# Feed-forward blocks of a two-layer hybrid decoder step: order of the TensorE passes in each slice's first output, and place of the sums of squares

## The reference

```python
def rms_norm(x, g):
    xf = x.astype(jnp.float32)
    y = xf * lax.rsqrt(jnp.mean(xf * xf, axis=-1, keepdims=True) + EPS)
    return (y * g.astype(jnp.float32)).astype(x.dtype)

def sqrelu_mlp(h, w_up, w_down):
    return jnp.square(jax.nn.relu(h @ w_up)) @ w_down

xp = xp + op
xp = xp + sqrelu_mlp(rms_norm(xp, norm_mlp[i]), mlp_w_up[i], mlp_w_down[i])
```

## Time and profile before

| | before |
|---|---|
| median of 3 runs | 2505.18 us (2504.93 to 2505.47) |
| profiled execution, its own time | 2504.88 us |
| its span | 2502.7 us |
| PE busy | 2414.7 us, 96% |
| DVE busy | 1013.8 us, 41% |
| ACT busy | 574.8 us, 23% |
| POOL busy | 107.1 us, 4% |
| DMA, mean | 61 GB/s |
| mean granted clock of PE | 0.987 |

### The profile page before, as it was taken

The page is one execution under the profiler, slowest core; times in us unless marked ns, Lnnn a source line. Parts: engine busy times, 40 slices in busy tenths (PEclk is TensorE's granted clock), DMA queues, the critical chain, the costliest instruction groups (busy, mean ns, idle before and its releaser), DMA issues.

```text
span 2502.7 us, 35278 instructions
## 1 busy us (share of the span) xinstructions
PE 2414.7 (96%) x15189; PEld 2339.8 (93%) x15189; DVE 1013.8 (41%) x1391; ACT 574.8 (23%) x998; POOL 107.1 (4%) x121
## 2 busy tenths in 40 slices
PE   6997899999999999999999998999999999999998
PEld 6995689999999999999999998888999999999998
DVE  5346833533333334334622323644433333333333
ACT  5346832201101111102410014522110110110111
POOL 0003510000000000000000002200000000000000
PEclk9998999999999999999999999999999999999999
DMA  8522021111111111111221126432111111111111
GB/s 227 106 48 76 2 88 51 34 51 34 50 34 50 50 34 50 37 47 50 88 54 51 34 76 181 122 109 84 34 50 50 34 50 42 42 50 34 50 34 70
DMA packets 122486, 153.86 MB, mean 61 GB/s; under 512 B 24797, under 2 KB 97273, under 8 KB 122120
## 3 DMA queue, kind: packets, MB, share of 16 engines
q1 hardware_dynamic: 116732, 139.33, 18.4%
q0 software_dynamic: 2832, 13.08, 1.8%
q10 hardware_dynamic: 2844, 0.34, 0.1%
HBM read 127.01 MB, written 27.76 MB: 62 GB/s over the span
## 4 chain that ended last, share of the span: by engine, by line
PE 90%; DVE 5%; ACT 2%; DMA 1%; issue 1%; POOL 1%; SPq 0%; POOLq 0%; DVEq 0%
PE ps L299 38%; PE ps L305 20%; PE ps L285 8%; PE ps L288 8%; PE ps L286 8%; DVE act_lo L1181 1%; DVE relu_sq L1177 1%; DVE relu L1170 1%; DMA raw<-in_attn_w_qkv 1%; PE ps L700 1%; PE ps L718 1%; ACT prob L774 1%; PE ps L1064 1%; PE ps L1691 0%; PE ps L1065 0%
## 5 line engine op out<-in xcount | busy, mean ns | idle before, releaser
L1188 DVE TENSOR_TENSOR x<-x,ps 128x1074 f32<-128x1074 f32 (+1 forms) x128 | 161.8, 1264 | 481.7 <-PE ps L305 481.5
L299 PE MATMUL ps<-act_hi,w_hi 128*128 128x358 f32 (+1 forms) x1536 | 335.5, 326 | 16.5 <-DVE act_lo L1181 16.5
L257 ACT ACTIVATE w_hi<-raw 128x1024 fp32r<-128x1024 f32 x180 | 187.1, 1049 | 677.3 <-PE ps L305 503.4
L299 PE MATMUL ps<-h_hi,w_hi 128*128 128x358 f32 (+1 forms) x1536 | 335.1, 326 | 0.0
L299 PE MATMUL ps<-act_hi,w_lo 128*128 128x358 f32 (+1 forms) x1536 | 334.3, 325 | 0.0
L299 PE MATMUL ps<-h_hi,w_lo 128*128 128x358 f32 (+1 forms) x1536 | 333.6, 325 | 0.0
L285 PE MATMUL ps<-h_hi,w_hi 128*128 128x358 f32 (+1 forms) x864 | 287.7, 333 | 10.0 <-DVE w_lo L262 8.2
L286 PE MATMUL ps<-h_lo,w_hi 128*128 128x358 f32 (+1 forms) x864 | 283.3, 328 | 0.0
L299 PEld LDWEIGHTS ps<-act_hi,w_hi 128*128 128x128 f32 x1536 | 263.2, 189 | 21.2 <-DVE act_lo L1181 21.2
L305 PE MATMUL ps<-act_lo,w_hi 128*128 128x358 f32 (+1 forms) x1536 | 269.5, 324 | 0.0
L1170 DVE SCALAR_TENSOR_TENSOR relu<-ps,rstd 128x1074 f32<-128x1074 f32 (+1 forms) x64 | 81.1, 1267 | 460.8 <-PE ps L305 460.8
(11 more groups left out here) (305 smaller groups left out, 2337.8 us busy)
## 6 DMA issues: line engine op xcount, KB each, us to landing
raw<-in_mlp_w_up SPq DMA_DIRECT2D x32, 1024.0 KB, 5.5
raw<-in_mlp_w_down SPq DMA_DIRECT2D x32, 1024.0 KB, 5.1
raw<-in_mlstm_w_in SPq DMA_DIRECT2D x12, 1024.0 KB, 5.3
scratch_x<-x SPq DMA_DIRECT2D x1, 4296.0 KB, 19.7
x<-scratch_x SPq DMA_DIRECT2D x8, 537.0 KB, 5.9
scratch_x<-x POOLq DMA_DIRECT2D x1, 4296.0 KB, 12.9
scratch_og<-stage POOLq DMA_DIRECT2D x8, 528.0 KB, 3.4
x<-scratch_x SPq DMA_DIRECT2D x8, 528.0 KB, 4.7
```

The source lines that it names most:

```text
L257: nc.scalar.activation(unit_view(w_hi, slot, down), raw_unit(j, rslot, down), ACT.Copy).then_inc(w_hi_ready, 1)
L299: nc.tensor.matmul(ps[:, bank + g, 0:width], w_block(w, slot, k, kc, cols), hi[:, k, g * width:g * width + width], start=start and i == 0, ...
L1188: nc.vector.tensor_tensor(view(x[:, o, :]), view(x[:, o, :]), ps[:, out_banks(n):out_banks(n) + 3, 0:w], ALU.add).then_inc(out_free, 1)
```

## The change

Four things change, in both layers. In the first down output of each slice (o = 4) the low passes of blocks 0 to 2 stand before the wait for block 3. The first up output of slice 0 is taken out of the loop as `first_up_pe`, with the three sums of squares inside its low passes, behind blocks 1, 3 and 5. The rest of slice 0 is written out once, and PE's loop runs over slices 1 to 7. DVE writes the low parts of blocks 0 and 1 before it adds the last square.

```diff
-            norm_acc_dve(dve, m, KC - 1)
             dve.wait_ge(out_ready, n0 + KC)
             for c in range(KC):
+                if c == 2:
+                    norm_acc_dve(dve, m, KC - 1)
                 norm_lo_dve(dve, m, c, x, h_hi, h_lo)
...
+        def first_up_pe(pe, layer, u0, n0, h_hi, h_lo):
+
+            m = 2 * layer + 1
+            _, w, _ = mlp_cols(layer)
+            pe.wait_ge(w_lo_ready, u0 + 1)
+            pe.wait_ge(out_free, n0 - 1)
+            for k in range(KC):
+                pe.wait_ge(norm_hi, KC * m + k + 1)
+                pass_hi(u0 % 4, k, 8, slice(0, P), out_banks(n0), h_hi, k == 0, w)
+            for k in range(KC):
+                pe.wait_ge(norm_lo, KC * m + k + 1)
+                last = pass_lo(u0 % 4, k, 8, slice(0, P), out_banks(n0), h_lo, k == KC - 1, w)
+                if k in (1, 3, 5):
+                    norm_pe(pe, m, k // 2)
+            last.then_inc(out_ready, 1)
...
-                    for k in range(deep):
-                        if o == 0:
-                            pe.wait_ge(norm_hi, KC * (2 * layer + 1) + k + 1)
+                    cols, bank = slice(P * c, P * c + P), out_banks(n0 + o)
+                    early = deep - 1 if o == 4 else deep
+                    for k in range(early):
                         if o == 4:
                             pe.wait_ge(act_split, i * 4 + (ups + k + 1))
...
+                    for k in range(early):
+                        last = pass_lo(slot, k, deep, cols, bank, lo, k == deep - 1, w)
+                    for k in range(early, deep):
+                        pe.wait_ge(act_split, i * 4 + (ups + k + 1))
+                        pass_hi(slot, k, deep, cols, bank, hi, False, w)
+                        last = pass_lo(slot, k, deep, cols, bank, lo, True, w)
                     last.then_inc(out_ready, 1)
...
-            for g in range(3):
-                norm_pe(pe, 1, g)
-            with pe.Fori(0, SLICES) as i:
+            first_up_pe(pe, 0, U_MLP0, N_MLP0, h_hi, h_lo)
+            mlp_slice_pe(pe, 0, U_MLP0, N_MLP0, 0, h_hi, h_lo, 1)
+            with pe.Fori(1, SLICES) as i:
                 mlp_slice_pe(pe, 0, U_MLP0, N_MLP0, i, h_hi, h_lo)
```

More of the change, by code:

```diff
@@ L1197, in mlp_slice_dve, with mlp_slice_pe @@
                 norm_lo_dve(dve, norm[0], KC - 1, *norm[1:])
-        def mlp_slice_pe(pe, layer, u0, n0, i, h_hi, h_lo):
+        def first_up_pe(pe, layer, u0, n0, h_hi, h_lo):
[12 more added lines that the diff above has]
+            last.then_inc(out_ready, 1)
+        def mlp_slice_pe(pe, layer, u0, n0, i, h_hi, h_lo, skip=0):
             ups = 4 * SLICES * layer
             _, w, _ = mlp_cols(layer)
-            for j in range(8):
+            for j in range(skip, 8):
                 pe.wait_ge(w_lo_ready, i * 8 + (u0 + j + 1))
@@ L1208, in mlp_slice_pe @@
                     pe.wait_ge(out_free, i * 12 + (n0 + o - 1))
-                    for k in range(deep):
-                        if o == 0:
-                            pe.wait_ge(norm_hi, KC * (2 * layer + 1) + k + 1)
+                    cols, bank = slice(P * c, P * c + P), out_banks(n0 + o)
+                    early = deep - 1 if o == 4 else deep
+                    for k in range(early):
                         if o == 4:
                             pe.wait_ge(act_split, i * 4 + (ups + k + 1))
[L1214 to L1218, removed]
+                        pass_hi(slot, k, deep, cols, bank, hi, k == 0, w)
+                    for k in range(early):
[4 more added lines that the diff above has]
+                        last = pass_lo(slot, k, deep, cols, bank, lo, True, w)
                     last.then_inc(out_ready, 1)
@@ L2097, in out_dve @@
                 add_x_dve(dve, N_OUT + c, c, x2, 3)
-            norm_acc_dve(dve, 3, KC - 1)
             dve.wait_ge(out_ready, N_OUT + KC)
             for c in range(KC):
+                if c == 2:
+                    norm_acc_dve(dve, 3, KC - 1)
                 norm_lo_dve(dve, 3, c, x2, h_hi2, h_lo2)
@@ L2347, in _ @@
             out_pe(pe)
-            for g in range(3):
-                norm_pe(pe, 3, g)
-            with pe.Fori(0, SLICES) as i:
+            first_up_pe(pe, 1, U_MLP1, N_MLP1, h_hi2, h_lo2)
+            mlp_slice_pe(pe, 1, U_MLP1, N_MLP1, 0, h_hi2, h_lo2, 1)
+            with pe.Fori(1, SLICES) as i:
                 mlp_slice_pe(pe, 1, U_MLP1, N_MLP1, i, h_hi2, h_lo2)
```

## The result

| | before | changed |
|---|---|---|
| median | 2505.32 us (4 runs) | 2468.28 us (2467.12 to 2469.46, 4 runs) |
| ratio to before | 1 | 0.9851, 95% interval 0.9839 to 0.9864 |
| profiled execution | 2504.88 us | 2467.12 us |

What follows compares the result with a forecast made beforehand. PE bounds the kernel (busy 96%, 90% of the chain), so only its idle or slow time can go: 20.7 + 7.9 + 7.0 = 35.6 us off 2504.88, a median of 2469.5 us, range 2466.5 to 2475.5.

Steps and rivals of the forecast that it cites:

- Part 1: First down output of each slice: low passes ahead of the fourth block close the act_lo gap, 20.7 us gained.
- That is 0.29 us to spare: Layer 0's first down output: PE reaches block 3 at 496.63 us, its operand released at 496.34.
- Rival B: The slice's act_lo wait is only shortened: about 0.5 us a slice stays, 8 us in all, 2477.5 us; chance 0.05.
- Part 2: Entries to the feed-forward: first up unit with its sums runs without waits, gaining 7.9 us in layer 0, 7.0 in layer 1.
- So none waits, with 0.25 us as the smallest margin: Layer 0's entry: every operand is ready before PE; tightest is low block 7, reached 0.25 us after h_lo 7.
- about 1.2: Layer 0's entry: each old sum of squares takes about 1.2 us, where 0.6 is expected after the change.
- free to come until 458.0: Behind layer 0's entry: rstd may come as late as 458.0 us, 10 us after the third sum, without a cost.
- Part 3: Slice 0 written out, PE's loop over seven slices: entering the loop costs 0, with 1 us each as the other end.
- the rule on branches: PE's loop: a taken branch outside the pages at hand forces a fetch, so the old jump back should have stalled.
- The profiled run's sum: Whole kernel: profiled execution of 2504.88 us less the 35.6 us gain gives 2469.3 us.
- the forecast 1715.5: Layer 1's entry: second up unit starts at 1733.78 less 18.3 us won by then, 1715.5 us.

Runs made afterwards that it cites:

- runs with two and one block: Changed kernel with the low passes of two blocks, or of one, instead of three ahead of the fourth block's wait: 2477.14 and 2482.28 us.
- the filled wait: Kernel before with 27 matmuls that nobody reads put ahead of the sums of squares at each layer's entry: 2502.45 us, ratio 0.9988.
- the entries alone: Changed kernel with the first down output's passes put back in the old order: median 2492.38 us, ratio 0.9947.

## Why the prediction was right

**Part 1** was taken at 20.7 us; alone it measured 20.3. Its step "That is 0.29 us to spare" decided. In the changed kernel act_lo ends at 488.29 and the signal takes 0.05, and PE comes at 488.63: 0.29. The runs with two and one block confirm it from the other side: the operand was there 4.15 us behind the output's first matmul whatever PE did ahead of it. Rival B falls.

**Part 2** was taken at 7.9 and 7.0 us and came out at 7.9 and 7.1. "So none waits, with 0.25 us as the smallest margin": h_lo 7 is done at 440.12 + 7.57 = 447.69, and PE comes to it at 448.65 less three spacings, 448.16, so the margin was 0.5. One reading was off without touching the sum: the old sums took 1.07 us each, not about 1.2. That the order of DVE is what keeps it is shown by turning it, which costs 2.0 us at each entry where 1.9 and 1.8 were expected. rstd, said to be free to come until 458.0, was ready at 449.56.

**Part 3** was taken as free, and is: even without any jump on PE the time is that of the changed kernel's runs. The prediction expected a fetch, and so a stall, at the old jump back if the rule on branches held; by the packets nothing was fetched there, so there was nothing to stall for.

**What was not foreseen.** The forecast median was 1.2 us above the first measurement, 0.4 below the second (2469.89) and 0.4 above the third (2469.15). That it fell inside 1.2 us of each is in part luck, since single runs of the changed kernel lie up to 5.5 us apart. The profiled run's sum was 2.2 us off (2469.3 against 2467.12), of which 1.7 is the shorter stretch at 1.2 GHz between the layers. For the same reason layer 1's second up unit starts at 1713.71, not at the forecast 1715.5. The prediction took all that lies outside the changed places as fixed; in this kernel the time moves by 2.3 to 5.5 us from run to run, with the same code. Smaller expectations missed: the run with two blocks (7.2 instead of 3 to 5 us), the filled wait (3.4 instead of 4.8), and the entries alone, whose median hides a spread of 5.3 us.

## What to carry to other kernels

When the bounding engine waits for the last of several operands, order its work so that everything that needs only the earlier ones stands ahead of the wait, and count: the wait is covered when that work's end passes the operand's time, which can be read as a distance from the event that starts the operand's own chain. Then look at the engine that feeds it, since an order there that was harmless (a sum ahead of eight low parts) becomes the bound as soon as the consumer arrives earlier. And a wait on TensorE can cost more than its length: the one of 4.96 us here cost some 2.4 us on top, since matmuls behind it ran at half the clock.

## What the runs showed of the hardware

- A wait of 4.96 us at layer 0's entry was followed by work at 1.2 GHz: mean clock 0.84 over 21.6 us; with 27 matmuls (4.4 us) in it, 1.00. The Trainium skill, TensorE: Matmul & The Clock Gate, Why this matters for your kernels, warns of idle gaps between bursts of matmuls for this reason; the trace agrees, and by the run with the wait filled the price was 2.4 us for this one.
- The clock also fell with PE busy 28.00 of 28.00 us, in or right behind a row of 18 float32 products with 4 moving columns each, and by an amount that differed from run to run of the same code (0.94, 0.88, 0.82). Spread among full matmuls in groups of 1.9 us they left it at 1.00 in both traces. Busy time in the profile is therefore no proof of the upper clock.
- A wait for 0.2 us on PE (arrival after 3.95 us, operand at 4.15) left no entry in PE's list of waits, and cost 0.35 us in each slice; the idle time of the weight loads showed 0.35.
- A loop body of 576 matmuls and as many weight loads was fetched once (4.5 packets), and neither the entry to the loop nor the jump back left a gap between matmuls 0.16 us apart.
